# Three edits to a one-core mixer and mixture-of-experts kernel: the scan's row loads and VectorE order, the first stage's loop order, the spreads of the output projection

## The reference

```python
mod = silu(c) @ w_ada + b_ada              # six rows of 1024: shifts, scales, gates
h = rms_norm(x) * (1 + sc1) + sh1
u, z, xbc, dt_raw = split(h @ w_in)        # 256, 768, 1792, 12 columns
xbc = silu(causal_depthwise_conv(xbc))     # 4 taps
# ssd_scan: 8 chunks of 128 tokens, 12 heads of 64, 4 groups, state 128
a_cs = cumsum(dt * a)                      # per chunk and head
decay = exp(a_cs[l] - a_cs[s]) for s <= l  # per head 128 x 128
y_diag = ((C B^T) * decay) @ (x * dt)
states = B^T @ (x * dt * exp(a_cs[-1] - a_cs))
state  = state * exp(a_cs[-1]) + states    # from chunk to chunk
y = y_diag + (C @ state_before) * exp(a_cs) + x * d_skip
y = group_rms_norm(y * silu(z)) * norm_w   # 4 groups over 768 channels
mix = concat(y_pool, y) @ w_out
x = x + g1 * mix
```

## Time and profile before

| | us |
|---|---|
| median of 3 runs | 2445.2 (2443.64 to 2447.38) |
| the profiled execution | 2441.31 |
| its span, first to last instruction | 2439.5 |
| first stage, up to the scan's first DMA | 0 to 324.98 |
| scan | 324.98 to 448.6 |
| output projection | 448.6 to 577 |
| PE busy over the span | 2155.8 (88%) |

### The profile page before, as it was taken

How to read it: one execution, slowest core, us unless ns; L and a number is a source line. 1 busy time by engine, 2 the same in 40 slices (tenths; PEclk the granted TensorE clock), 3 DMA queues, 4 the chain that set the end, 5 groups by cost and what they waited for, 6 DMA issues and landing times. The chain is left out here.

```text
span 2439.5 us, 43265 instructions
## 1 busy us (share of the span) xinstructions
PE 2155.8 (88%) x15880; PEld 1613.3 (66%) x15880; DVE 1218.0 (50%) x1530; ACT 821.3 (34%) x1198; POOL 562.2 (23%) x381
## 2 busy tenths in 40 slices
PE   5799978897567879889959898989999999999998
PEld 4588856586323435444538786768888888888887
DVE  7777345434336768777855528823332122311344
ACT  5112145201425758767843006722100001000123
POOL 1323301130000000000013462213333233332343
PEclk8899978898669889999977999999999999999999
DMA  7532123425999996999853220011111111111113
GB/s 278 218 139 99 33 104 122 166 78 233 372 410 388 360 344 228 393 333 341 315 202 112 69 82 1 1 52 52 43 52 43 52 51 43 52 43 52 51 52 121
DMA packets 106179, 376.90 MB, mean 154 GB/s; under 512 B 8092, under 2 KB 19196, under 8 KB 105724
## 3 DMA queue, kind: packets, MB, share of 16 engines
q1 hardware_dynamic: 87628, 332.94, 37.7%
q10 hardware_dynamic: 13008, 23.07, 2.5%
q0 software_dynamic: 5472, 19.93, 2.3%
HBM read 344.39 MB, written 31.51 MB: 154 GB/s over the span
## 5 line engine op out<-in xcount | busy, mean ns | idle before, releaser
L1618 PE MATMUL moe_hu<-x_res,moe_xt 128*32 128x256 f32 x5120 | 338.7, 408 | 79.0 <-DVE moe_xt L1534 52.3
L1512 DVE COPY x_res<-moew_raw 128x2048 f32 x243 | 270.1, 1135 | 186.0 <-DMA moew_raw<-in_w 116.8
L1618 PEld LDWEIGHTS moe_hu<-x_res,moe_xt 128*32 128x32 f32 x5120 | 163.5, 116 | 210.7 <-issue 88.8
L241 PE MATMUL ff_acc<-ff_yh,ff_w_hi 128*128 128x512 f32 x704 | 274.4, 390 | 0.0
L241 PE MATMUL ff_acc<-ff_yh,ff_w_lo 128*128 128x512 f32 x704 | 273.9, 389 | 0.0
L241 PE MATMUL ff_acc<-ff_yl,ff_w_hi 128*128 128x512 f32 x704 | 273.9, 389 | 0.0
L1512 ACT ACTIVATE x_res<-moew_raw 128x2048 f32 (+1 forms) x121 | 197.2, 1629 | 106.6 <-DMA moew_raw<-in_w 67.3
L209 POOL CAST ff_w_hi<-ff_w_raw 128x1024 fp32r<-128x1024 f32 (+1 forms) x82 | 81.9, 998 | 548.2 <-PE ff_acc L241 548.2
L241 PE MATMUL ff_acc<-xh,ff_w_hi 128*128 128x512 f32 x480 | 188.8, 393 | 7.9 <-DVE ff_w_lo L225 7.2
L211 POOL TENSOR_TENSOR ff_w_lo<-ff_w_raw,ff_w_hi 128x1024 fp32r<-128x1024 f32 (+1 forms) x82 | 188.7, 2301 | 6.6
L241 PE MATMUL ff_acc<-xl,ff_w_hi 128*128 128x512 f32 x480 | 187.9, 392 | 0.0
(11 more groups left out here) (390 smaller groups left out, 3721.8 us busy)
## 6 DMA issues: line engine op xcount, KB each, us to landing
moew_raw<-in_w SPq DMA_DIRECT2D x192, 1024.0 KB
ff_w_raw<-in_w_up SPq DMA_DIRECT2D x44, 512.0 KB, 3.5
mid_w_raw<-in_w_qkv SPq DMA_DIRECT2D x24, 512.0 KB, 3.5
in_w_raw<-in_w_in SPq DMA_DIRECT2D x23, 512.0 KB, 3.5
xbc<-in_w_ada SPq DMA_DIRECT2D x20, 512.0 KB, 7.9
y_scratch<-acc_sq ACTq DMA_DIRECT2D x80, 128.0 KB
ff_w_raw<-in_w_down SPq DMA_DIRECT2D x16, 512.0 KB, 3.5
x_res<-in_w_ada SPq DMA_DIRECT2D x14, 512.0 KB, 4.4
```

Of the source, the lines that this page charges most:

```text
L241: m = pe.matmul(o, w[:, b, k * P:(k + 1) * P], x[:, k, h:h + HALF], start=(k == 0 and t == 0), stop=(k == kt - 1 and t == 2))
L1512: m = e.activation(to, src, ACT.Copy) if k == "act" else e.tensor_copy(to, src)
L1618: m = e.matmul(hu[u % 2][rows(j), 0:2 * FW].rearrange("p (a f) -> p a f", a=2), xt[:, t, rows(u)], w[:, :, FW * j:FW * (j + 1)], start=(t ...
```

## The change

First stage: DVE's loop step begins with the convolutions and ends with `ada_dve`; SP's step loads weight tile 2i+4, then the four w_ada rows, then weight tile 2i+5. Scan: the row is loaded once, into `m`; ACT's `exps` first writes the exponent of `m` into `ce` and then applies Relu to `m` in place; DVE calls `decay_c(c + 1)` after the state and `x_dt(c + 1)` instead of before `gated`. Output projection: one `spread(j)` writes both token halves with four products in four row quarters, and spreads 1 to 5 are issued between the first products, whose order is now by channel tile and then half; ACT converts the first weights before it loads its table; DVE forms the root before it splits the second weight tile; POOL waits for `inv` before its work.

```diff
                     with e.Fori(0, N_SILU) as i:
+                        g.load(e, i, 4, 0, W[2 * i + 4])
                         ada_load(e, i)
-                        for b in range(2):
-                            g.load(e, i, 4, b, W[2 * i + (4 + b)])
+                        g.load(e, i, 4, 1, W[2 * i + 5])
...
                     with st.dve.loop(N_SILU) as i:
-                        ada_dve(e, i)
                         for b in range(2):
...
+                        ada_dve(e, i)
                     ada_finish(e)
...
                         e.dma_start(m[c % 2], row).then_inc(s_bm[c % 2], 16)
-                        e.dma_start(ce[c % 2], row).then_inc(s_bc[c % 2], 16)
...
                     def exps(c):
                         b = c % 2
+                        spread(e, c)
+                        wait(e, "y", c - 2)
+                        done(e.activation(ce[b], m[b], ACT.Exp), "exp_bc")
                         wait(e, "dte_arg", c)
+                        wait(e, "exp_bc", c)
                         for h in range(HEADS):
...
-                        spread(e, s_bc, c)
-                        done(e.activation(ce[b], ce[b], ACT.Exp), "exp_bc")
...
                     for c in range(NCH):
-                        if c + 1 < NCH:
-                            decay_c(c + 1)
                         wait(e, "y", c)
...
                         if c + 1 < NCH:
                             x_dt(c + 1)
+                            decay_c(c + 1)
...
-            first = [(h, k) for h in range(2) for k in range(POOL_T)] + [(h, POOL_T + j) for h in range(2) for j in range(SSD_T)]
+            first = [(h, k) for k in range(KT) for h in range(2)]
...
-            steps = [(h, j) for h in range(2) for j in range(SSD_T)]
+            steps = [(h, j) for j in range(SSD_T) for h in range(2)]
...
                     st.pool.start(e)
+                    st.wait(e, st.dve, "inv")
...
-                    for n, (h, j) in enumerate(steps):
-                        if n >= 2:
-                            st.wait(e, st.dve, "normed%d%d" % steps[n - 2])
+                    def spread(j):
+                        if j:
+                            st.wait(e, st.dve, f"normed1{j - 1}")
                         for q in range(2):
-                            rows = slice(64 * h + 32 * q, 64 * h + 32 * q + 32)
-                            m = e.matmul(total[n % 2][:, q, :], member_t[rows, j, :], rstd[rows, :],
-                                         start=True, stop=True, tile_position=(64 * h + 32 * q, 0))
-                        st.pe(m, f"spread{h}{j}")
+                            for h in range(2):
+                                rows = slice(64 * h + 32 * q, 64 * h + 32 * q + 32)
+                                m = e.matmul(total[h][:, q, :], member_t[rows, j, :], rstd[rows, :],
+                                             start=True, stop=True, tile_position=(64 * h + 32 * q, 0))
+                        st.pe(m, f"spread{j}")
...
                                 h, k = first[n]
+                                if h == 0 and 0 < k < SSD_T:
+                                    spread(k)
...
-                    e.preload_act_table(ACT.Sqrt)
                     e.wait_ge(self.s_w_first, 32)
...
+                    e.preload_act_table(ACT.Sqrt)
```

More of the change, by code:

```diff
@@ L896, in ssd @@
             s_fill, s_zeros, s_state0, s_skip = (st.sem(n) for n in ("fill", "zeros", "state0", "skip"))
-            s_bm, s_bc = [st.sem(f"bcast_m{b}") for b in range(2)], [st.sem(f"bcast_ce{b}") for b in range(2)]
-            spread = lambda e, sems, c: e.wait_ge(sems[c % 2], 16 * (c // 2) + 16)
+            s_bm = [st.sem(f"bcast_m{b}") for b in range(2)]
+            spread = lambda e, c: e.wait_ge(s_bm[c % 2], 16 * (c // 2) + 16)
             zeros = self.x[:, SSD_T + 1, 0:HALF]
@@ L1039, in arguments @@
                         b = c % 2
-                        spread(e, s_bm, c)
+                        spread(e, c)
                         wait(e, "xdte", c - 2)
@@ L1178, in route @@
                         return m
+                    spread(0)
                     first_products()
@@ L1215, in _, with split @@
                     e.sem_inc(g.s_split, 2)
-                    for b in range(2):
+                    def split(b):
                         e.wait_ge(g.s_first, b + 1)
                         e.tensor_tensor(g.lo[:, b, :], self.w_first[:, b, :], g.hi[:, b, :].bitcast(F32), ALU.subtract).then_inc(g.s_split, 1)
+                    split(0)
                     st.wait(e, st.pe, "group_sum")
@@ L1222, in _ @@
                     st.dve(e.reciprocal(rstd[:, :], rstd[:, :]), "inv")
+                    split(1)
                     def low(h, j):
@@ L1227, in _ @@
                     for n, (h, j) in enumerate(steps):
-                        st.wait(e, st.pe, f"spread{h}{j}")
+                        st.wait(e, st.pe, f"spread{j}")
                         yq = y(h, j).rearrange("p (b x) -> p b x", b=2)
-                        st.dve(e.scalar_tensor_tensor(yq, yq, self.col("ssd_norm_w", j), total[n % 2], ALU.mult, ALU.mult), f"normed{h}{j}")
+                        st.dve(e.scalar_tensor_tensor(yq, yq, self.col("ssd_norm_w", j), total[h], ALU.mult, ALU.mult), f"normed{h}{j}")
                         if n:
```

## The result

The changed kernel takes 2459.9 us (median of 7 executions, 2452.0 to 2476.7) against 2445.2 for the kernel before (7 executions beside it). The ratio is 1.0072, 95% interval 1.0048 to 1.0096: **slower by 0.5 to 1.0%**. I had forecast 2449.8 and called "no change" and "slower" nearly even. The sign of the leaning was right, the size was three to four times too small, and behind it stand three errors that partly cancel, so that the sum came nearer than its terms.

A forecast was written before the change was run, and what follows sets the result against it. It took TensorE (PE) to bound the first stage from 94.27 us and no engine to be full in the scan; -16.4 (first stage) + 24.2 (scan) - 3.2 (output projection) = +4.6 us, median 2449.8, eight in ten within 2436 to 2462.

The forecast's parts named there:

- the clock term: Scan: TensorE's pauses lower its clock, so an output pass costs 1.9 us more a chunk, between 0 and 3.98.
- base: Scan: the new circle from output to output, 14.3 us a chunk before port and clock costs, against 13.68 before.
- all later passes recovered: Scan: reason for a clock cost of 1.9 us, nearer chunk 2's 1.3 than chunk 0's 3.98.
- the port term: Scan: POOL's xdte beside VectorE's first ce product costs that product 1.0 us a chunk, bounds 0 and 1.3.
- the opening claim: First stage: PE is the bound from 94.27 us on, so time won or lost before shifts the rest.
- (e): Output projection: rival that spreads overlap, total -2 us, 2443; chance 0.05.
- (b): Scan: rival that the port wait fails to appear, chunks of 16.2 us, total -2.4, 2442.8; chance 0.12.
- (c): Scan: rival that the clock stays low through every output pass, chunks of 19.3 us, total +19, 2464; chance 0.11.
- the main case: Whole kernel: scan chunks of 17.2 us, total +4.6 us, range 2444 to 2455; chance 0.45.
- (a): Scan: rival that the clock stays high, chunks of 15.3 us, total -8.7, 2436.5; chance 0.12, without port wait 0.04.
- (d): Output projection: rival that the clock stays low through the interleaved spreads, total +14 us, 2459; chance 0.09.

The follow-up runs named there:

- filler_late: Changed kernel plus 12 unread matmuls a chunk in TensorE's pause and POOL's xdte(c) waiting for m(c) too; 2432.5 us, ratio 0.9949.
- pe_filler: Changed kernel plus 12 unread matmuls in each of seven chunks, ahead of the waits for ce and m; 2441.7 us, ratio 0.9975.
- xdte_late: Changed kernel with POOL's xdte(c) waiting for m(c) too, so not beside VectorE's multiplication of ce by C; 2462.7 us, ratio 1.0058.
- first_only: Kernel before with only the first-stage edits (SP's load order, ada_dve last in VectorE's loop); 2442.8 us, ratio 0.9977.
- two_parts: Changed kernel with the whole scan of the kernel before; 2430.4 us, ratio 0.9921.
- old_order: Changed kernel with decay_c(c + 1) back ahead of gated(c), single row load and early exponent kept; 2434.1 us, ratio 0.9945.
- raw_first: Changed kernel with the scan of before, and both copies ahead of both silus in ScalarE's first-stage loop; 2419.4 us, ratio 0.9884.
- order_only: Kernel before with one edit, decay_c(c + 1) behind x_dt(c + 1) instead of ahead of gated(c); 2480.3 us against 2447.1, ratio 1.0135.

## Why the prediction was wrong, step by step

**Scan: mechanism right, the clock term mis-sized.** Forecast +24.2, measured +35.8 in the profiled execution. The seven chunks by the experiments: base 14.4 (filler_late's 101.00 us by seven; 14.2 without its one long chunk) against my 14.3; port 0.90 against 1.0; **clock 3.2 against 1.9**. In us over seven chunks the first two came to within 1 of the forecast; the clock term was 22.3 against 13.3. The step that failed is the reason that I gave for the lower half of the range: "all later passes recovered". Those passes of before had work straight ahead of them; in the new order each pass has a pause of 3.54 us or more ahead, as only chunk 0 had before (2.80), so chunk 0 was the row to size by. It says 3.98 at a pause of 2.80, which bounds the 3.2 measured. Besides, chunk 0 itself became 2 us longer, where I had 0.4 gained: 1.4 of it ahead of its pass (its `ce` multiplication took 3.24, beside `xdte`), the rest in the pass, all of it at the low clock. I had priced the port term for the later chunks alone.

The time also spreads: seven passes of one execution took 7.48 to 10.65 us, and the changed kernel's seven executions range over 25 us, those of before in the same comparison over 6.5. With the clock held by pe_filler, eleven executions range over 9. I take the clock for the cause of the spread; the profile of one execution a kernel does not show it. A forecast to 5 us was hard to have for this kernel.

I weighed the Trainium skill (TensorE: Matmul & The Clock Gate, section "HAM oscillation — how this bites in real kernels") against the rows, and took the rows' side: the clock would fall. That was right. The page describes a pause before each block that makes each block begin cold, "Every single K-tile."; the trace agrees: all seven passes ran below 1.00 on average (0.50 to 0.77), the one shown of pe_filler, with the pause filled, at 1.00, and I should have counted every chunk. One long gap was not needed: in xdte_late six passes had a pause of 2.58 us ahead, and five of them ran at 0.50 to 0.55.

**First stage: the gap closed as forecast, and two thirds of it did not arrive.** Forecast -16.4, measured -6, outside the bounds of 14 to 16.8. TensorE's side came out: the first convolution ended at 77.7 (78.0 forecast), the gap went, and the tile after it ran at the high clock. At the last tile of the loop TensorE was still 15.2 us ahead of before (222.87 for 238.06). Behind it came the 6.82 us wait for the softplus chain: the next tile began 7.5 us earlier than before (242.62 for 250.12) and took 12.72 us at a mean clock of 0.87, where it had taken 11.17, and 5.95 were left. The step that failed is "At its end four L411 (4.6 us) stand before the softplus chain, which waits for ACT anyway", and with it the opening claim that a shift of TensorE's work "shifts all the rest of that stage". ScalarE and VectorE hand each other four things a pass (copy, convolution, silu, copy), with the four L411 between, and the softplus chain hangs on this circle, not on TensorE. In the changed kernel a pass of it takes 21.76 us, exactly what TensorE's two tiles take, and from the fourth pass on ScalarE's copies stay 8.1 and 9.0 us behind the ends of their tiles, to the last pass.

The equal periods are hardly an accident, for 21.76 us is not the circle's own length: in the kernel before, right behind the gap, it made a pass in 17.80 us (L668 at 93.21 and 111.01) and had caught up with TensorE, to 0.13 us, one copy later. In the changed kernel GpSimd splits a weight tile as soon as TensorE ends one, and VectorE's instruction beside the split ends 1.08 us behind the split's end, in all 14 splits of the loop. Lines of GpSimd and VectorE at the first of them:

```profile
71.05 2.72 POOL L211 TENSOR_TENSOR in_w_lo<-in_w_raw,in_w_hi 128x1024 fp32r<-128x1024 f32 x1
```
```profile
71.68 3.17 DVE L818 SCALAR_TENSOR_TENSOR in_wrk<-in_raw,cols,in_wrk 128x1024 f32<-128x1024 f32 x1 [0.17 <-DVE in_wrk L814]
75.01 2.71 DVE L818 SCALAR_TENSOR_TENSOR in_wrk<-in_raw,cols,in_wrk 128x1024 f32<-128x1024 f32 x2 [0.17 <-DVE in_wrk L818]
```

One such instruction takes 3.17 us beside the split; the two behind it take 2.71 together. So the splits, which follow TensorE's tiles, pace VectorE, and the circle keeps its lag. first_only, two_parts and old_order show the same lags of 8.1 and 9.0 us. This pacing is read from the traces; no run takes the splits away.

What does get rid of the lag is raw_first: with both copies ahead of both silus, the only edit against two_parts, each copy follows its tile's end by 0.1 us, and the load leaves at 309.31, against 308.6 forecast. Of the 16.4 us, 15.7 were there to be had, by another edit.

**Output projection: right in kind, the spreads mis-sized.** Forecast -3.2, measured -9.3. The earlier start came as forecast (first spread 5.57 us into the stage, 7.57 before). The step that failed: "The row shows two quarters at 1.05 us with no overlap to be seen". A row of the timeline that merges four records shows only their common length. The single records of the spread at 457.50 show what is inside: the two quarters' first matmuls begin at 457.496 and 457.503, their second ones at 457.923 and 457.930. The quarters ran side by side, and 1.06 us is the time of one quarter. The length of a record (0.63 us) does not tell this by itself, since products of all 128 rows, which take turns, have it too and begin 0.43 us apart (kernel before):

```profile
471.24 0.63 PE L1155 MATMUL mixout_acc<-xl_mix,mixout_w_hi 128*128 128x512 f32 x1
471.66 0.63 PE L1155 MATMUL mixout_acc<-xh_mix,mixout_w_lo 128*128 128x512 f32 x1
```

Four quarters cost 0.64 to 0.77 us where the mean clock was 0.81 to 1.00, and 1.16 at the low one (raw_first), not 2.1. Six double spreads then cost some 4 instead of 9.5 us. A second term was mis-sized too: the clock rose during the second double spread (mean 0.82, from 487.99 to 488.74), behind two groups of three products and not seven, some 3 us less than my 4.3. From the first spread to L1188 it is 29.01 us, for my 36.6. No run separates these two terms. The stage up to L1188 is 34.58 us, from 45.43: 10.85 less, at my bound (11); up to the expert load 9.25 of it are left. By the rule that I set aside, the Trainium skill (TensorEngine Tiling (Array Packing), section "Key Properties": "Tiles operate independently"), the term was -8. This trace agrees with the rule: four quarters begin within 0.02 us.

**The rivals.** None happened alone. (e), overlapping spreads, did. (b) did not: the port wait appears in every chunk and goes with xdte_late. (c) was the right neighbour: the chunks took 18.5 us, between the main case's 17.2 and its 19.3. (a) and (d) are excluded. What I lacked was the rival for the first stage, that the gap closes and the gain stays behind: I had listed only that the gap stays.

**The errors together**: +10.4 (first stage), +11.6 (scan) and -6.1 (output projection) on the profiled execution. By the runs of the single edits (order_only, first_only, out_only) the parts are +33, -5.6 and -11.7 us for my +24.2, -16.4 and -3.2. By the medians it is 2459.9 against 2449.8: that the whole came within some 10 us is owed to errors of both signs.

## What to carry to other kernels

Closing a gap on one engine moves that engine. Ask of each later stage which engine's chain it hangs on, whether that chain can catch up, and, when two engines' loops show equal periods, what ties them together. When work that ran beside TensorE is moved to where TensorE waits for it, price every repetition with the clock of the row that has the same pause ahead of it, not with the mean over rows that have none. And before reading "no overlap" from a merged row, look at when its single records start: their lengths alone can't tell.

## What the runs showed of the hardware

Added TensorE work made a kernel faster: 84 matmuls that nobody reads took the changed kernel's ratio to before from 1.0072 to 0.9975, some 24 us, since the passes behind them, to judge by the profiled execution, ran in 6.1 us and not in 7.5 to 10.65. A busy pass of 10.64 us can run at 1.2 GHz from end to end; being busy did not bring the clock back within it. Shortening a pause from 3.54 to 2.58 us did not help the clock: the seven passes took 10.0 us on average for 8.95.

GpSimd's 1.47 us instruction beside a VectorE product with two SBUF operands cost VectorE 0.95 us in six of eight chunks and 1.28 in chunks 0 and 2, and delaying GpSimd by one wait gave all of it back to VectorE at no cost to GpSimd's reader. In the first stage GpSimd's 2.7 to 3.3 us split beside VectorE's convolution did more than cost time: by the traces it tied VectorE's loop to TensorE's tiles, at a constant lag.
